# A two-layer gated attention trunk on one core: the third head pair's values move to another buffer, and VectorE instead of GpSimd scales the probabilities

## The chip, the cores and the metric

The kernel runs on one NeuronCore of a Trainium2 chip. The metric is the device time of the whole program in microseconds (us); lower is better. Engines are named as in the profile: PE (TensorE, matrix products; PEld is its weight load), DVE (VectorE), ACT (ScalarE), POOL (GpSimd), SP (the queue that issues the weight loads). Each engine works through its own instruction list in order, and an instruction waits until the semaphores it names have reached their counts.

## The reference: what is computed

Two layers act on 256 tokens of width 1024, in float32. Each layer is a half-step SwiGLU, a gated mixer, and another half-step SwiGLU. The mixer adds a pooling branch and an eight-head causal attention. The attention, cut to what matters:

```python
q = (rms_norm(q_lat, q_norm) @ w_uq).reshape(B, S, N_HEADS, QK_DIM)       # 128 + 64 rotary per head
kv = (rms_norm(kv_lat, kv_norm) @ w_ukv).reshape(B, S, N_HEADS, 128 + 128)
k_nope, v = kv[..., :128], kv[..., 128:]
for blk in range(S // 128):                                               # causal, 128 queries at a time
    s = (q_nope @ k_nope^T + q_rope @ k_rope^T) * QK_DIM ** -0.5
    p = softmax(where(mask, s, min))
    outs.append(p @ v[:, :k_end])
```

## The kernel before, in words

**Precision by splitting.** Every product is made of three passes over fp32r operands: high by high, high by low, low by high (`passes`). So each operand exists twice. ACT copies it rounded to fp32r (the high part, `high`, `split`), and DVE subtracts that from the original (the low part, `low`, `split`). Weights arrive in a ring of three slots `raw`, which ACT turns into `w_hi` and DVE into `w_lo`, one group `m` at a time (`split_mix(L, m)`); "split m" below is that step. A slot of `w_hi` is free again when PE has used the group three earlier.

**The attention by head pairs.** Eight heads are four pairs `p` = 0 to 3. For each pair PE makes the queries (`pair_queries`, parts QN and QRO) and the keys and values (`pair_keys`, parts KN and VV) in PSUM banks 2 to 5, one bank per part. ACT and DVE take each part out with `operands(L, p, part)`. PE then makes the scores (`pair_scores`, banks 6 and 7); DVE masks them and takes row maxima (`maxima`); ACT makes the exponentials and their row sums (`softmax`); `normalise` divides by the sums; PE transposes the probabilities into banks 0 and 1 (`turn_probs`); ACT and DVE copy these out (`probs`); PE multiplies by the values into bank 0 (`pair_values`); ACT and DVE copy the result to `oT` (`heads_out`). The rotary part of a query goes from PSUM to `xs` on ACT (`rope_copy`), is multiplied on POOL (`rope`), and goes on to ACT and DVE (part QRO).

**Order.** The lists of all engines are written out by hand and interleave these steps. The pieces of PE's list around the change are `pair_queries(2)`, `pair_keys(2)`, `turn_probs(0)`, `pair_scores(1)`, `pair_queries(3)`, `pair_values(0)`, `pair_keys(3)`, `turn_probs(1)`, `pair_scores(2)`, the first half of the pooling projection, `pair_values(1)`, its second half, `turn_probs(2)`, `pair_scores(3)`, and so on. Three waits of PE matter:

- `turn_probs(p)` waits for `prob_done`, count p+1 (`normalise(p)` is done), and for p above 0 also for `o_lo`, count p: DVE has read bank 0 in `heads_out(p-1)`.
- `pair_keys(3)` writes the values of pair 3 into bank 5, and first waits until DVE has taken the values of pair 2 out of it (`free(L, 3, VV)`).
- `pair_values(p)` waits for `prob_lo` and the low part of the values.

**Buffers.** `pair(p, part)` lies in `xT` for even p and in `pair1` for odd p. The values of pair 2 therefore overwrite those of pair 0, and ACT may copy them only when `pair_values(0)` is done (`pv_done`). `oT` holds the outputs of all eight heads; its last two heads are written by `heads_out(3)`, at the end of the attention.

Of the kernel before, what the change touches and what calls it, by code (L numbers as in the profile page):

```python
# [27 lines left out]
ALU = mybir.AluOpType  # L28
AX = mybir.AxisListType

P = 128
S, D, DEPTH = 256, 1024, 2
TB = S // P
KD = D // P
HEADS, NOPE, ROPE, VD = 8, 128, 64, 128
# [19 lines left out]
PAIRS = HEADS // 2  # L55
# [28 lines left out]
QN, QRO, KN, VV = range(4)  # L84

PART_ORDER = [(p, part) for p in range(2) for part in (QN, KN, VV, QRO)]
PART_ORDER += [(2, QN), (2, KN), (2, QRO), (3, QN), (2, VV), (3, KN), (3, QRO), (3, VV)]


GU_BANK, TR_BANK = 4, 6  # L90
# [49 lines left out]
def trunk(nc, x_in, positions, gains, ffn1_up, ffn1_down, w_in, b_gate, pool_maps, pool_scale,  # L140
          w_pool_proj, q_latent_norm, w_uq, kv_latent_norm, w_ukv, w_attn_proj, w_out,
          ffn2_up, ffn2_down, c_ident, c_causal, c_window, c_inv_count, c_rotary, out):
    with ExitStack() as ctx:
        def sb(name, shape, dt=F32):
            return ctx.enter_context(nc.sbuf_tensor(name, shape, dt))
# [17 lines left out]
        oT = sb("oT", [P, 2, HEADS, S], F32R)  # L163
# [27 lines left out]
        rot_t = rot[:, S:2 * S].rearrange("p (t c n) -> p t c n", t=TB, c=2)  # L191

        def pair(p, part):
            buf = (xT, pair1)[p % 2]
            return buf[:, :, 2 * part:2 * part + 2, :]

# [2 lines left out]
        LSQ, LMS, LRS = 6, 10, 14  # L199
        SMX, SNM, SSUM, SINV = 18, 22, 26, 28  # L200
        stat2 = sb("stat2", [P, 2, 16])
        half_neg, neg_one = sb("half_neg", [P, 2]), sb("neg_one", [P, 4])
        table_junk = sb("table_junk", [P, 1])
        pos_col_i, pos_col = sb("pos_col_i", [P, TB], I32), sb("pos_col", [P, TB])

# [249 lines left out]
        def _(pool):  # L455
# [2 lines left out]
                return pool.dma_start(dst, src.to_broadcast(list(dst.shape))).then_inc(landed, 16)  # L458

            pool.memset(half_neg[:, :], -0.5).then_inc(exponent_set, 1)  # L460
            pool.memset(neg_one[:, :], -1.0).then_inc(exponent_set, 1)
            def load_tables():

                pool.wait_ge(first_landed[1][3], 16)
# [59 lines left out]
                tensor(angle[:, :], angle[:, :], sign, ALU.mult)  # L524
                rot_op(pool.tensor_copy(window[:, :], window_f))

            def normalise(L, p):
                row, st = scores[:, p % 2, :], stat2[:, p % 2, :]
                pool.wait_ge(exp_done.sem, exp_done.upto(L, p + 1))
                pool.tensor_tensor(st[:, 12:16], st[:, 8:12], neg_one[:, :], ALU.pow).then_inc(inv_done.sem, 1)  # L530
                pool.wait_ge(inv_done.sem, inv_done.upto(L, p + 1))
                for cols, i, n in ((slice(0, 2 * S), 12, S), (slice(2 * S, 3 * S), 14, P)):
                    v = row[:, cols].rearrange("p (h n) -> p h n", h=2)
                    last = pool.tensor_tensor(v, v, st[:, i:i + 2].unsqueeze(2).to_broadcast([P, 2, n]), ALU.mult)
                last.then_inc(prob_done.sem, 1)

            def rope(L, p):
                both = rope_rows(p).rearrange("p (h n) -> p h n", h=2)
                pool.wait_ge(rope_in.sem, rope_in.upto(L, p + 1))
                pool.tensor_tensor(both, both, rot_f.unsqueeze(1).to_broadcast([P, 2, S]),  # L540
                                   ALU.mult).then_inc(rope_done.sem, 1)
# [15 lines left out]
                    pool.wait_ge(normed[h].sem, normed[h].upto(L, normed_count(s, TB - 1)))  # L557
                broadcast(gain[:, :], gains[bass.ds(L * 3 + s + 1, 1), :], gain_landed)

            pool.wait_ge(exponent_set, 2)  # L560
            def rest(L):

                broadcast(lat_gain[:, 0:QR], q_latent_norm[bass.ds(L, 1), :], latg_landed)
                broadcast(lat_gain[:, QR:QR + KVR], kv_latent_norm[bass.ds(L, 1), :], latg_landed)
                for t in range(TB):
                    broadcast(gates[:, t, :], b_gate[bass.ds(L, 1), :], bias_landed)
                next_gain(L, 0)
                second_half(L, 1)
                next_gain(L, 1)
                norm_rsqrt(L, 1)  # L570
                for i in range(2):
                    pool.wait_ge(lat_ms.sem, lat_ms.upto(L, i + 1))
                    rs = stat[:, LRS + 2 * i:LRS + 2 * i + 2]
                    rsqrt(rs, stat[:, LMS + 2 * i:LMS + 2 * i + 2], 2, lat_rstd)

                    pool.wait_ge(lat_rstd.sem, lat_rstd.upto(L, i + 1))
                    pool.tensor_tensor(rs, rs, stat[:, NRS:NRS + TB], ALU.mult).then_inc(lat_scale.sem, 1)
                rope(L, 0)
                rope(L, 1)
                normalise(L, 0)  # L580
                rope(L, 2)
                normalise(L, 1)
                rope(L, 3)
                normalise(L, 2)
                normalise(L, 3)
                second_half(L, 2)
                next_gain(L, 2)
                norm_rsqrt(L, 2)
# [32 lines left out]
        def _(act):  # L621
# [85 lines left out]
            def operands(L, p, which):  # L707
                for part in which:
                    src = psum[:, 2 + part, :]
                    if part == QRO:  # L710
                        high(L, rope_done, p + 1, flat(pair(p, part), 0), rope_rows(p), part_hi)
                        continue
                    if part == VV and p >= 2:

                        act.wait_ge(pv_done.sem, pv_done.upto(L, p - 1))
                    part_products(act, L, p, part)
                    act.activation(flat(pair(p, part), 0), src, ACT.Copy).then_inc(part_hi.sem, 1)
# [47 lines left out]
            def mixer(L):  # L765
# [46 lines left out]
                operands(L, 2, (QN, ))  # L812
                rope_copy(L, 2)
                split_mix(L, 22)
                operands(L, 2, (KN,))
                probs(L, 0)
                split_mix(L, 23)
                operands(L, 2, (QRO,))
                softmax(L, 1)
                operands(L, 3, (QN,))  # L820
                rope_copy(L, 3)
                operands(L, 2, (VV,))
                heads_out(L, 0)
                operands(L, 3, (KN,))
                split_mix(L, 24)
# [83 lines left out]
        def _(dve):  # L909
# [16 lines left out]
            def split_mix(L, m):  # L926
                if m < MIX_GROUPS:
                    split(L, (MIX0 + m) // RING, m % RING, m)
                else:
                    split(L, FFN2_0 // RING, m - MIX_GROUPS)  # L930
# [255 lines left out]
            def operands(L, p, which):  # L1186
                for part in which:
                    src = psum[:, 2 + part, :]
                    if part == QRO:
                        src = rope_rows(p)  # L1190
                    low(L, part_hi, part_count(p, part), flat(pair(p, part), 1), src, flat(pair(p, part), 0), part_lo)

            def maxima(L, p):
# [11 lines left out]
                dve.wait_ge(max_done.sem, max_done.upto(L, p + 1))  # L1205
                dve.tensor_scalar(st[:, 4:8], st[:, 0:4], -SCALE, None, ALU.mult).then_inc(bias_done.sem, 1)

            def probs(L, p):
                low(L, prob_hi, p + 1, small_T[:, 1, 0:3 * S], banks(0)[:, 0:3 * S], small_T[:, 0, 0:3 * S], prob_lo)

            def heads_out(L, p):
                o = oT[:, :, 2 * p:2 * p + 2, :]
                low(L, o_hi, p + 1, flat(o, 1), psum[:, 0, :], flat(o, 0), o_lo)
# [20 lines left out]
            def mixer(L):  # L1234
# [47 lines left out]
                operands(L, 1, (QRO,))  # L1282
                operands(L, 2, (QN,))
                split_mix(L, 22)
                operands(L, 2, (KN,))
                probs(L, 0)
                maxima(L, 1)
                split_mix(L, 23)
                operands(L, 2, (QRO,))
                operands(L, 3, (QN,))  # L1290
                operands(L, 2, (VV,))
                heads_out(L, 0)
                operands(L, 3, (KN,))
                split_mix(L, 24)
                probs(L, 1)
                maxima(L, 2)
                split_mix(L, 25)
                operands(L, 3, (QRO, VV))
                heads_out(L, 1)
                dve.wait_ge(gate_sig.sem, gate_sig.upto(L, 4 * TB))  # L1300
# [1 line left out]
                probs(L, 2)  # L1302
                maxima(L, 3)
                split_mix(L, 26)
                heads_out(L, 2)
                probs(L, 3)
                gate_a(L, 1)
# [408 lines left out]
```

## Time and profile before

| | |
|---|---|
| median of 3 runs | 1135.0 us (1133.81 to 1137.13) |
| the profiled execution: its time, and the span of its trace | 1135.97 us, 1134.2 us |
| PE busy in the span | 1114.0 us (98%) |
| DVE busy | 649.9 us (57%) |
| ACT busy | 538.0 us (47%) |
| POOL busy | 127.4 us (11%) |
| attention of layer 0, of layer 1 | about 282 to 345 us, about 838 to 901 us |

The span is the time from the first to the last instruction of the trace; the execution's own time is 1.8 us more. A busy share says how full an engine is, not whether it is waited for. The attention is done once in each layer, and the rows of the two layers repeat each other, so only those of layer 0 are shown.

### The profile page before, as it was taken

The page shows a single profiled execution, that of the slowest core. Times are in us where ns is not written, and L with a number is a line of the kernel's source. Part 1 is how long each engine was busy: PE and PEld are TensorE (multiplying, and loading weights), DVE is VectorE, ACT ScalarE, POOL GpSimd, SP SyncE. Part 2 cuts the span into 40 slices and gives each one's busy share as a digit, 9 for nine tenths or more (in the row PEclk, how much of TensorE's full clock was granted, in tenths as well). Part 3 has the DMA queues.
Part 4 walks back from the last instruction along what each step waited for, and adds up shares of the span by engine and source line. Part 5 has one row for each costly group of instructions (what it writes and reads, how often), then busy time and mean ns, then how long its engine had stood idle before and what let it go on. Part 6 is the DMA issues. An engine that isn't in the chain of part 4 may idle for free.

```text
span 1134.2 us, 14607 instructions
## 1 busy us (share of the span) xinstructions
PE 1114.0 (98%) x5472; PEld 937.6 (83%) x5472; DVE 649.9 (57%) x610; ACT 538.0 (47%) x615; POOL 127.4 (11%) x122
## 2 busy tenths in 40 slices
PE   7999999999999999999999999999999999999997
PEld 5788888988988888888878888888899888888886
DVE  4555455676776554544565545556568576454454
ACT  5444434554863443444444443446567435344442
POOL 4960000200230100000020000011002101000000
PEclk9999999999999999999999999999999999999999
DMA  9667554554544655556557565538435355655650
GB/s 301 229 221 248 190 185 153 191 189 125 189 149 149 202 187 186 184 185 191 186 203 258 184 193 185 185 102 278 141 129 196 121 180 185 201 185 185 188 181 37
DMA packets 140487, 208.59 MB, mean 184 GB/s; under 512 B 5185, under 2 KB 103617, under 8 KB 139937
## 3 DMA queue, kind: packets, MB, share of 16 engines
q1 hardware_dynamic: 137456, 196.69, 53.3%
q0 software_dynamic: 2128, 9.80, 2.6%
q10 hardware_dynamic: 864, 1.57, 0.4%
q8 instruction: 26, 0.43, 0.2%
q14 instruction: 13, 0.10, 0.0%
HBM read 207.00 MB, written 1.05 MB: 183 GB/s over the span
## 4 chain that ended last, share of the span: by engine, by line
PE 93%; DVE 3%; ACT 3%; POOL 1%; issue 0%; POOLq 0%; ACTq 0%; DVEq 0%
PE psum L1341 30%; PE psum L1343 30%; PE psum L1342 29%; PE psum L1409 2%; PE psum L1359 1%; DVE w_lo L917 1%; PE psum L1684 1%; ACT scores L735 1%; ACT w_hi L630 1%; ACT xs L723 0%; POOL xs L544 0%; DVE xT L917 0%; PE psum L1551 0%; ACT xT L650 0%; DVE stat L1203 0%
## 5 line engine op out<-in xcount | busy, mean ns | idle before, releaser
L917 DVE TENSOR_TENSOR w_lo<-raw,w_hi 128x2048 fp32r<-128x2048 f32 (+6 forms) x212 | 436.6, 2066 | 266.6 <-ACT w_hi L630 264.3
L630 ACT ACTIVATE w_hi<-raw 128x2048 fp32r<-128x2048 f32 (+5 forms) x204 | 355.2, 1748 | 181.6 <-PE psum L1343 166.0
L1341 PE MATMUL psum<-w_hi,xT 128*128 128x512 f32 (+2 forms) x992 | 389.7, 393 | 7.4 <-DVE scores L1086 4.7
L1343 PE MATMUL psum<-w_hi,xT 128*128 128x512 f32 (+2 forms) x992 | 383.5, 387 | 0.0
L1342 PE MATMUL psum<-w_lo,xT 128*128 128x512 f32 (+2 forms) x992 | 382.8, 386 | 0.0
L1341 PEld LDWEIGHTS psum<-w_hi,xT 128*128 128x128 f32 x992 | 186.8, 188 | 44.6 <-DVE w_lo L917 9.2
L1343 PEld LDWEIGHTS psum<-w_hi,xT 128*128 128x128 f32 x992 | 186.5, 188 | 37.5
L1342 PEld LDWEIGHTS psum<-w_lo,xT 128*128 128x128 f32 x992 | 186.9, 188 | 34.4
L1341 PE MATMUL psum<-w_hi,small_T 128*128 128x512 f32 x352 | 137.6, 391 | 0.0
L1343 PE MATMUL psum<-w_hi,small_T 128*128 128x512 f32 x352 | 137.0, 389 | 0.0
L1342 PE MATMUL psum<-w_lo,small_T 128*128 128x512 f32 x352 | 137.0, 389 | 0.0
L650 ACT ACTIVATE small_T<-psum 128x512 fp32r<-128x512 f32 (+1 forms) x52 | 32.9, 632 | 173.7 <-PE psum L1409 161.4
L917 DVE TENSOR_TENSOR small_T<-psum,small_T 128x512 fp32r<-128x512 f32 (+1 forms) x52 | 38.1, 732 | 97.7 <-ACT small_T L650 97.4
L679 ACT ACTIVATE scores<-psum,stat 128x256 f32<-128x256 f32 x88 | 41.6, 474 | 102.9 <-PE psum L1343 102.9
L544 POOL TENSOR_TENSOR xs<-x,gain 128x512 f32<-128x512 f32 x12 | 20.7, 1733 | 593.6 <-DVE x L911 583.9
L1343 PEld LDWEIGHTS psum<-w_hi,small_T 128*128 128x128 f32 x352 | 66.1, 188 | 13.8
L1342 PEld LDWEIGHTS psum<-w_lo,small_T 128*128 128x128 f32 x352 | 66.1, 188 | 13.5
L1341 PEld LDWEIGHTS psum<-w_hi,small_T 128*128 128x128 f32 x352 | 66.1, 188 | 13.5
L1086 DVE SCALAR_TENSOR_TENSOR scores<-psum,stat,scores 128x256 f32<-128x256 f32 x88 | 42.0, 480 | 37.3 <-ACT scores L679 37.3
L650 ACT ACTIVATE xT<-psum 128x512 fp32r<-128x512 f32 x32 | 19.2, 600 | 59.5 <-PE psum L1359 59.4
L917 DVE TENSOR_TENSOR xT<-psum,xT 128x512 fp32r<-128x512 f32 x44 | 30.1, 688 | 29.4 <-ACT xT L650 27.3
L1341 PE MATMUL psum<-latT,w_hi 128*128 128x256 f32 x104 | 29.7, 286 | 0.0
(173 smaller groups left out, 947.0 us busy)
## 6 DMA issues: line engine op xcount, KB each, us to landing
raw<-ffn_up_dram SPq DMA_DIRECT2D x172, 512.0 KB, 4.7
raw<-ffn_down_dram SPq DMA_DIRECT2D x44, 1024.0 KB, 4.9
raw<-w_in_dram SPq DMA_DIRECT2D x20, 1024.0 KB, 5.2
raw<-w_attn_proj_dram SPq DMA_DIRECT2D x8, 1024.0 KB, 5.1
raw<-w_out_dram SPq DMA_DIRECT2D x8, 1024.0 KB, 5.0
raw<-w_uq_dram SPq DMA_DIRECT2D x8, 576.0 KB, 4.1
gates<-b_gate_dram POOLq DMA_DIRECT2D x4, 1024.0 KB, 8.0
raw<-w_ukv_dram SPq DMA_DIRECT2D x8, 512.0 KB, 4.0
```

Source lines behind the costliest of these rows:

```text
L544: pool.tensor_tensor(xs[:, t, half(h)], x[:, t, half(h)], gain[:, half(h)], ALU.mult).then_inc(normed[h].sem, 1)
L630: last = act.activation(dst(w_hi[:, r, :]), src(raw[:, r, :]), ACT.Copy)
L650: act.activation(dst, src, ACT.Copy).then_inc(done.sem, 1)
L679: act.activation(silu_sb[:, t, :], psum[:, GU_BANK + t, 0:CH], ACT.Silu, scale=rstd(t)).then_inc(silu_done.sem, 1)
L735: last = act.activation(row[:, cols], src, ACT.Exp, scale=SCALE, bias=st[:, 4 + i:5 + i], accum_out=st[:, 8 + i:9 + i])
L917: return dve.tensor_tensor(dst, a, b, ALU.subtract)
L1086: dve.scalar_tensor_tensor(out=act_sb[:, t, :], in0=psum[:, GU_BANK + t, CH:2 * CH], scalar=rstd(t), in1=silu_sb[:, t, :], op0=ALU.mult, o ...
L1341: nc.tensor.matmul(dst, a_hi, b_hi, start=first, stop=False)
L1342: nc.tensor.matmul(dst, a_hi, b_lo, start=False, stop=False)
L1343: return nc.tensor.matmul(dst, a_lo, b_hi, start=False, stop=last)
L1359: last = nc.tensor.transpose(dst[:, k * P:(k + 1) * P], src[:, k * P:(k + 1) * P], ident[:, :])
L1409: last = nc.tensor.transpose(psum[:, TR_BANK, k * S + t * P:k * S + (t + 1) * P], act_sb[:, t, k * P:(k + 1) * P], ident[:, :])
```

## The change

The values of pair 2 get a place of their own in the last two heads of `oT`, and are copied out of PSUM together with the keys of pair 2, with no wait for `pair_values(0)`. `normalise` moves from POOL's list to DVE's: POOL had one power of -1 over 4 columns and two broadcast products (512 and 256 columns); DVE has one reciprocal over 4 columns and four products by a per-row scalar (256, 256, 128, 128 columns). In each layer that is four calls. Everything that issues a DMA is as before.

```diff
-PART_ORDER += [(2, QN), (2, KN), (2, QRO), (3, QN), (2, VV), (3, KN), (3, QRO), (3, VV)]
+PART_ORDER += [(2, QN), (2, KN), (2, VV), (2, QRO), (3, QN), (3, KN), (3, QRO), (3, VV)]
...
         def pair(p, part):
+            if (p, part) == (2, VV):
+                return oT[:, :, HEADS - 2:HEADS, :]
             buf = (xT, pair1)[p % 2]
...
 # POOL
-            def normalise(L, p):
-                row, st = scores[:, p % 2, :], stat2[:, p % 2, :]
-                pool.wait_ge(exp_done.sem, exp_done.upto(L, p + 1))
-                pool.tensor_tensor(st[:, 12:16], st[:, 8:12], neg_one[:, :], ALU.pow).then_inc(inv_done.sem, 1)
-                pool.wait_ge(inv_done.sem, inv_done.upto(L, p + 1))
-                for cols, i, n in ((slice(0, 2 * S), 12, S), (slice(2 * S, 3 * S), 14, P)):
-                    v = row[:, cols].rearrange("p (h n) -> p h n", h=2)
-                    last = pool.tensor_tensor(v, v, st[:, i:i + 2].unsqueeze(2).to_broadcast([P, 2, n]), ALU.mult)
-                last.then_inc(prob_done.sem, 1)
...
-                rope(L, 0)
-                rope(L, 1)
-                normalise(L, 0)
-                rope(L, 2)
-                normalise(L, 1)
-                rope(L, 3)
-                normalise(L, 2)
-                normalise(L, 3)
+                for p in range(PAIRS):
+                    rope(L, p)
...
 # ACT
-                    if part == VV and p >= 2:
+                    if part == VV and p == 3:
                         act.wait_ge(pv_done.sem, pv_done.upto(L, p - 1))
...
                 split_mix(L, 22)
-                operands(L, 2, (KN,))
+                operands(L, 2, (KN, VV))
                 probs(L, 0)
...
                 rope_copy(L, 3)
-                operands(L, 2, (VV,))
                 heads_out(L, 0)
...
 # DVE
+            def normalise(L, p):
+                row, st = scores[:, p % 2, :], stat2[:, p % 2, :]
+                dve.wait_ge(exp_done.sem, exp_done.upto(L, p + 1))
+                dve.reciprocal(st[:, 12:16], st[:, 8:12]).then_inc(inv_done.sem, 1)
+                dve.wait_ge(inv_done.sem, inv_done.upto(L, p + 1))
+                for i, cols in enumerate(ROWS):
+                    last = dve.tensor_scalar(row[:, cols], row[:, cols], st[:, 12 + i:13 + i], None, ALU.mult)
+                last.then_inc(prob_done.sem, 1)
...
                 split_mix(L, 22)
-                operands(L, 2, (KN,))
+                normalise(L, 0)
+                operands(L, 2, (KN, VV))
                 probs(L, 0)
                 maxima(L, 1)
                 split_mix(L, 23)
+                normalise(L, 1)
                 operands(L, 2, (QRO,))
                 operands(L, 3, (QN,))
-                operands(L, 2, (VV,))
                 heads_out(L, 0)
...
                 split_mix(L, 25)
+                normalise(L, 2)
                 operands(L, 3, (QRO, VV))
                 heads_out(L, 1)
...
                 split_mix(L, 26)
+                normalise(L, 3)
                 heads_out(L, 2)
```

DVE's list of before, layer 0, from the rotary queries of pair 1 (`pair<-xs`) to the start of `maxima(1)`; the row with 1024 columns is split 22, `xT<-psum,xT` are the low parts of pair 2's queries and keys, `small_T` is `probs(0)`:

```order
L917 TENSOR_TENSOR pair<-xs,pair 128x512
L917 TENSOR_TENSOR xT<-psum,xT 128x512
L917 TENSOR_TENSOR w_lo<-raw,w_hi 128x1024
L917 TENSOR_TENSOR xT<-psum,xT 128x512
L917 TENSOR_TENSOR small_T<-psum,small_T 128x768
L1200 TENSOR_TENSOR psum<-psum,causal 128x2x128
```

The same place in the changed kernel, where `oT<-psum,oT` is the low part of pair 2's values:

```order
L901 TENSOR_TENSOR pair<-xs,pair 128x512
L901 TENSOR_TENSOR xT<-psum,xT 128x512
L901 TENSOR_TENSOR w_lo<-raw,w_hi 128x1024
L1195 RECIPROCAL stat<-stat 128x4
L1198 TENSOR_SCALAR scores<-scores,stat 128x256 x2
L1198 TENSOR_SCALAR scores<-scores,stat 128x128 x2
L901 TENSOR_TENSOR xT<-psum,xT 128x512
L901 TENSOR_TENSOR oT<-psum,oT 128x512
L901 TENSOR_TENSOR small_T<-psum,small_T 128x768
L1184 TENSOR_TENSOR psum<-psum,causal 128x2x128
```

`normalise(0)` now stands behind split 22 on DVE, and the copy of the values stands ahead of `probs(0)`.

ACT's list of before, layer 0, from the last exponentials of `softmax(1)` through the queries of pair 3 (`pair<-psum`), its rotary copy (`xs<-psum`), the values of pair 2 (`xT<-psum`), `heads_out(0)` (`oT<-psum`) and the keys of pair 3 to split 24:

```order
L735 ACTIVATE scores,stat<-psum,stat 128x128 x2
L717 ACTIVATE pair<-psum 128x512
L723 ACTIVATE xs<-psum 64x256 x4
L717 ACTIVATE xT<-psum 128x512
L650 ACTIVATE oT<-psum 128x512
L717 ACTIVATE pair<-psum 128x512
L630 ACTIVATE w_hi<-raw 128x2048
```

The same place in the changed kernel:

```order
L720 ACTIVATE scores,stat<-psum,stat 128x128 x2
L702 ACTIVATE pair<-psum 128x512
L708 ACTIVATE xs<-psum 64x256 x4
L635 ACTIVATE oT<-psum 128x512
L702 ACTIVATE pair<-psum 128x512
L615 ACTIVATE w_hi<-raw 128x2048
```

The copy of pair 2's values is gone from between `rope_copy(3)` and `heads_out(0)`.

DVE's list of the changed kernel from split 25 through `normalise(2)`, the rotary queries (`pair<-xs`) and values (`pair<-psum`) of pair 3, and `heads_out(1)`:

```order
L901 TENSOR_TENSOR w_lo<-raw,w_hi 128x2048
L1195 RECIPROCAL stat<-stat 128x4
L1198 TENSOR_SCALAR scores<-scores,stat 128x256 x2
L1198 TENSOR_SCALAR scores<-scores,stat 128x128 x2
L901 TENSOR_TENSOR pair<-xs,pair 128x512
L901 TENSOR_TENSOR pair<-psum,pair 128x512
L901 TENSOR_TENSOR oT<-psum,oT 128x512
```

Before, the reciprocal and the four products were not there, and the other four rows followed one another.

## Rows read from the trace of the kernel before

**Rows 1.** The page, part 1: busy us, share of the span, instructions.

```profile
PE 1114.0 (98%) x5472; PEld 937.6 (83%) x5472; DVE 649.9 (57%) x610; ACT 538.0 (47%) x615; POOL 127.4 (11%) x122
```

**Rows 2.** What PE waited for, whole span: us in total, times, longest.

```profile
PE psum L1341 <- DVE xT L917: 2.3, 3, 1.0
...
PE psum L1551 <- POOL scores L534: 1.3, 2, 0.7
```

**Rows 3.** Timeline, PE around `turn_probs(0)`: start, us; idle before, releaser.

```profile
302.55 0.28 PE L1343 MATMUL psum<-w_hi,latT 128*128 128x256 f32 x1
303.49 0.85 PE L1551 MATMUL psum<-ident,scores 128*128 128x128 f32 x6 [0.66 <-POOL scores L534]
```

**Rows 4.** Timeline, POOL: `normalise(0)` and `rope(2)`.

```profile
300.56 1.09 POOL L530 TENSOR_TENSOR stat<-stat,neg_one 128x4 f32<-128x4 f32 x1 [5.86 <-ACT scores L735]
301.73 1.61 POOL L534 TENSOR_TENSOR scores<-scores,stat 128x512 f32<-128x512 f32 x2
303.30 1.28 POOL L540 TENSOR_TENSOR xs<-xs,rot 128x512 f32<-128x512 f32 x1
```

**Rows 5.** Timeline, split 22 on ACT and on DVE.

```profile
302.42 1.06 ACT L630 ACTIVATE w_hi<-raw 128x1024 fp32r<-128x1024 f32 x1
...
303.51 2.15 DVE L917 TENSOR_TENSOR w_lo<-raw,w_hi 128x1024 fp32r<-128x1024 f32 x1 [1.05 <-ACT w_hi L630]
```

**Rows 6.** Timeline, `rope(0)` on POOL, and split 18 on DVE.

```profile
287.62 1.29 POOL L540 TENSOR_TENSOR xs<-xs,rot 128x512 f32<-128x512 f32 x1 [58.10 <-ACT xs L723]
...
288.66 1.33 DVE L917 TENSOR_TENSOR w_lo<-raw,w_hi 128x1024 fp32r<-128x1024 f32 x1 [3.35 <-ACT w_hi L630]
```

**Rows 7.** Groups of DVE by form: busy us, mean ns of one, idle before.

```profile
L1200 DVE TENSOR_TENSOR psum<-psum,causal 128x256 f32<-128x256 f32 x8 | 3.5, 433 | 3.7 <-PE psum L1343 3.7
...
L1206 DVE TENSOR_SCALAR stat<-stat 128x4 f32<-128x4 f32 x8 | 1.4, 170 | 0.3
L1143 DVE TENSOR_SCALAR xs<-psum,stat 128x64 f32<-128x64 f32 x4 | 0.9, 277 | 0.0
...
L914 DVE TENSOR_TENSOR xs<-xs,rot 128x128 f32<-128x128 f32 x2 | 0.6, 292 | 0.1
```

**Rows 8.** Timeline, PE and DVE around the values of pair 3.

```profile
312.88 0.28 PE L1343 MATMUL psum<-latT,w_lo 128*128 128x256 f32 x1
314.20 0.39 PE L1341 MATMUL psum<-w_hi,latT 128*128 128x256 f32 x1 [1.04 <-DVE xT L917]
...
315.74 0.82 PE L1551 MATMUL psum<-ident,scores 128*128 128x128 f32 x6
...
313.45 0.69 DVE L917 TENSOR_TENSOR xT<-psum,xT 128x512 fp32r<-128x512 f32 x1 [0.93 <-ACT xT L717]
```

**Rows 9.** Timeline, DVE: start of `maxima(1)`, and split 23.

```profile
307.10 0.43 DVE L1200 TENSOR_TENSOR psum<-psum,causal 128x256 f32<-128x256 f32 x1
...
309.04 2.28 DVE L917 TENSOR_TENSOR w_lo<-raw,w_hi 128x2048 fp32r<-128x2048 f32 x1
```

**Rows 10.** Timeline, ACT from `rope_copy(3)` to split 24.

```profile
311.24 1.56 ACT L723 ACTIVATE xs<-psum 64x256 f32<-64x256 f32 x4
312.82 0.60 ACT L717 ACTIVATE xT<-psum 128x512 fp32r<-128x512 f32 x1
313.32 0.59 ACT L650 ACTIVATE oT<-psum 128x512 fp32r<-128x512 f32 x1
...
314.27 1.93 ACT L630 ACTIVATE w_hi<-raw 128x2048 fp32r<-128x2048 f32 x1
```

**Rows 11.** Timeline, DVE: split 24, rotary queries of pair 3, `heads_out(1)`.

```profile
316.23 2.29 DVE L917 TENSOR_TENSOR w_lo<-raw,w_hi 128x2048 fp32r<-128x2048 f32 x1 [0.89 <-ACT w_hi L630]
...
323.46 0.69 DVE L917 TENSOR_TENSOR pair<-xs,pair 128x512 fp32r<-128x512 f32 x1
...
324.71 0.68 DVE L917 TENSOR_TENSOR oT<-psum,oT 128x512 fp32r<-128x512 f32 x1
```

**Rows 12.** Timeline, PE: `turn_probs(2)`.

```profile
326.15 0.87 PE L1551 MATMUL psum<-ident,scores 128*128 128x128 f32 x6
```

More of the change, by code:

```diff
@@ L201, in trunk @@
         stat2 = sb("stat2", [P, 2, 16])
-        half_neg, neg_one = sb("half_neg", [P, 2]), sb("neg_one", [P, 4])
+        half_neg = sb("half_neg", [P, 2])
         table_junk = sb("table_junk", [P, 1])
@@ L460, in _ @@
             pool.memset(half_neg[:, :], -0.5).then_inc(exponent_set, 1)
-            pool.memset(neg_one[:, :], -1.0).then_inc(exponent_set, 1)
             def load_tables():
@@ L558, in next_gain @@
                 broadcast(gain[:, :], gains[bass.ds(L * 3 + s + 1, 1), :], gain_landed)
-            pool.wait_ge(exponent_set, 2)
+            pool.wait_ge(exponent_set, 1)
             def rest(L):
```

## The prediction, written before the changed kernel ran

> **What bounds the kernel now.** I read the busy shares first: PE is busy 98% of the span, so time is lost or won only where PE stands still [rows 1]. The list of PE's waits then says what this change can touch. PE waits twice, once per layer, for GpSimd's scaled probabilities, 0.66 us each, and three times for DVE to take something out into `xT`; the longest two of these, 1.04 us each, are the values of pair 2 [rows 2]. The timelines put both in place: the first stands ahead of `turn_probs(0)` [rows 3], the second inside `pair_keys(3)`, ahead of its value products [rows 8]. Everything else on POOL, DVE and ACT is either behind PE or has to be proved late by working through their queues, which is what I do next. Both layers show the same pattern, so I work one layer and double it.
>
> **What the change removes.** The wait in `pair_keys(3)` goes: the values of pair 2 will be copied some six us before they are asked for. Its price is start to start. Without it the products would have followed at 312.88 + 0.12 = 313.00 (the pitch of such products is 0.12) instead of 314.20, which is 1.20. The twelve of them took 315.74 - 314.20 = 1.54 where twelve at pitch take 1.44, so the restart cost 0.10 more. Gain 1.30 per layer [rows 8]. On POOL, 1.09 + 1.61 us of work go away per pair [rows 4]; POOL is not waited for again, so this is worth nothing by itself. ACT loses one copy of 0.50 (start to start) between `rope_copy(3)` and split 24 and gains it back ahead of `probs(0)`, where ACT will be waiting for PE anyway [rows 10].
>
> **What the change adds: the first stall.** DVE works in order, and `normalise(0)` stands behind split 22. Split 22 cannot start before ACT has made its high part, which ends at 303.48, and it starts at 303.51 [rows 5]. By then POOL had already finished `normalise(0)`, at 301.73 + 1.61 = 303.34 [rows 4], and PE went on at 303.49 [rows 3]. In the new order the probabilities are ready only at 303.51 + (split 22) + N, with N the length of `normalise` on DVE.
>
> Split 22 took 2.15 us, beside `rope(2)` on POOL from 303.30 to 304.58 [rows 4, 5]. The same instruction took 1.33 as split 18 [rows 6]. In the new kernel `rope(2)` no longer queues behind `normalise(0)`. It starts when its input is copied, about 302.5, and ends about 303.8, so only 0.26 us overlap split 22. Split 18 overlapped `rope(0)` by as much (287.62 + 1.29 = 288.91 against 288.66) and still took 1.33 [rows 6]. I take 1.33. The Trainium skill ("SBUF — State Buffer", Terms) says that DVE and GpSimd share a port pair which one of them holds for a whole instruction while the other fully blocks; this fits the 2.15 of split 22, but by it split 22 would also lose these 0.26 us, which makes the sum about 0.5 us larger over two layers, and the row of split 18 does not bear that out.
>
> An instruction with no wait starts about 0.08 before the end of the one ahead (307.10 and its followers on DVE step so), so `normalise(0)` starts at 304.76.
>
> N is not in the trace. The reciprocal over 4 columns I take as the nearest row, a TENSOR_SCALAR over 4 columns, 0.17, plus 0.04 until its own semaphore lets the products go: 0.21. For the products the nearest rows are a product by a per-row scalar of 64 columns, 0.277, and mask additions of 256 columns from PSUM, 0.433; 128 columns from SBUF took 0.292 [rows 7]. I take the middle, 0.36, for 256 columns and 0.28 for 128. Start to start that is 0.28 + 0.28 + 0.20 + 0.28 = 1.04, so N = 1.25. Low end: all four at 0.277, N = 1.1. High end: 0.433 and 0.35, N = 1.5, and a reciprocal three times as long as that row gives 1.7; if it cost as much as POOL's power, 1.09 [rows 4], N would be 2.3. The Trainium skill ("VectorE: DVE Perf Modes", the perf-mode tier table) says that a fp32 tensor_scalar within SBUF runs at two elements per cycle; an estimate from that page is N = 1.0 and a sum of 4.1 us in place of the one below.
>
> PE starts 0.06 after DVE ends (313.45 + 0.69 = 314.14 against 314.20 [rows 8]). So `turn_probs(0)` starts at 304.76 + 1.25 + 0.06 = 306.07 where it was 303.49: **2.58 later** (1.33 + N). Nothing of PE's can move ahead of it, and nothing hides it. The 0.66 us wait is not removed but becomes about 3.2.
>
> **After it.** Minus 1.30 for the values leaves PE 1.28 late (0.03 + N) at `turn_probs(1)`, 317.02. That step needs two things. `maxima(1)` follows PE's scores and starts at 307.10 + 2.58; split 23 follows at 309.04 + 2.58 = 311.62 and takes 2.20 start to start [rows 9]; `normalise(1)` runs 313.82 to 315.07, the rotary queries and queries take 0.60 each, and `heads_out(0)` (0.68) ends at 316.87. PE could go at 316.93: just in time, by 0.09. Any N above 1.34 makes a small third stall here.
>
> **The second stall, at `turn_probs(2)`.** Here `o_lo` is what counts. ACT's chain from `softmax(1)` over `rope_copy(3)` to split 24 is gapless [rows 10]; it starts 2.58 later and is 0.50 shorter, so split 24 is 2.08 later on ACT and on DVE, where it starts at 318.31, because DVE waited for it before too (0.89 idle) [rows 11]. From there DVE has no gap up to the rotary queries of pair 3 at 323.46, now 325.54. Ahead of them now stands `normalise(2)` (its exponentials are done by then), N - 0.08 = 1.17 more, so `heads_out(1)` starts at 324.71 + 2.08 + 1.17 = 327.96, ends at 328.64, and PE can go at 328.70. It was 326.15 [rows 11, 12]: **2.55 later** (0.05 + 2N), where PE itself would only have been 1.28 late. The cover was 326.15 - 325.39 - 0.06 = 0.70, and it is used up. At `turn_probs(3)` split 26 and `normalise(3)` end about 337.7 and `heads_out(2)` about 338.3, where PE arrives at about 339.1: no stall. The rest of the layer follows PE, and nothing later absorbs a delay, since PE had no other wait there.
>
> **Sum.** 2.55 per layer, 5.1 for both. The profiled execution had a span of 1134.2 and a time of 1135.97, 0.97 above the median of the runs. The new span would be 1139.3, and the median 1135.0 + 5.1 = **1140.1**, or 0.45% slower. About 0.3% (3.4 us) is what a measurement of this kernel tells from no change. With N from 1.1 to 1.7 the cost is 4.5 to 6.9: 1139.5 to 1141.9.
>
> **The rivals.**
> - *Only the first stall counts.* If DVE makes up 1.3 us before `heads_out(1)` (say ACT reaches split 24 earlier than its gapless chain allows), the cost is 2 x 1.28 = 2.6 us: 1137.6, no measurable change. For it speaks that my cover of 0.70 rests on a chain of some fifteen steps; against it that these steps have no gaps now. Chance 0.15.
> - *Faster.* Both waits of PE vanish and DVE is in time. That gives 1.30 + 0.82 (303.49 against 302.55 + 0.12 [rows 3]) per layer, 4.2 us: 1130.8. It decides at `turn_probs(0)`: the change wins as soon as the probabilities are ready less than 1.30 after 303.49, at 304.79, with `heads_out(1)` in time as well. Split 22 alone ends at 304.84, so it needs ACT to deliver split 22 over 1.2 us earlier, and ACT's list ahead of that point is unchanged. Chance 0.05.
> - *The port stays in the way.* If split 22 still takes 2.15, 0.82 is added per layer: 6.7 us, 1141.7. The row of split 18 speaks against it. Chance 0.06.
> - *A slow reciprocal.* With N = 2.3 the cost is 4.65 per layer, 1144.3. Only the power on another engine points that way. Chance 0.05.
> - *The moves change nothing* because the in-order view is wrong somewhere: 1135. Chance 0.04.
>
> My own case keeps 0.65.
>
> **How the numbers follow.** Slower by over 0.3% means above 1138.4: my case nearly whole (0.62), the port and the reciprocal (0.11), minus what run-to-run spread takes: 0.70. Within 0.3%: the first rival, the last, and the low tail of mine: 0.24. Faster: 0.06. The range takes in the first rival's upper half and the port's case, 1137.3 to 1142.1.
>
> **What would show it.** The page of the changed kernel should show DVE's split 22 at about 1.33 us, PE's wait ahead of `turn_probs(0)` at about 3.2 us and released by DVE's `scores`, no wait inside `pair_keys(3)`, next to none at `turn_probs(1)`, and about 1.2 us at `turn_probs(2)` released by DVE's `oT`, in both layers. PE's waits on POOL's `scores` go from 1.3 us to none. If the products turn out at 0.28 or less for 256 columns, N is 1.1 or less and the cost falls toward 4; if split 24 on DVE is less than 2.08 late, the second stall shrinks. The prediction is wrong in sign only if `turn_probs(0)` starts before 304.8.

## The result, and the profile after

The changed kernel took 1144.68 us (median of 4 runs, 1142.86 to 1145.51) against 1134.4 for the kernel before: ratio 1.0083, interval 1.007 to 1.0095. Run again later beside the kernel before, six runs of the same kernel gave 1141.39, ratio 1.005 (1.0038 to 1.0063). The forecast was 1140.1 and 1.0045, with 1142.1 as the upper end. The direction was right and the cost too small, and two sets of runs of one kernel differ by 3 us. TensorE's clock turns out to be behind the first, and, as far as profiles and granted clocks show, behind the second too.

The profile page of the changed kernel, its span and part 1, the row that answers to [rows 1]:

```profile
span 1143.7 us, 14620 instructions
...
PE 1118.3 (98%) x5472; PEld 942.6 (82%) x5472; DVE 656.1 (57%) x650; ACT 537.1 (47%) x615; POOL 104.5 (9%) x97
```

PE's busy time rose by 4.3 us although it executes the same 5472 products. That is not waiting: some products took longer. What PE waited for, in total, times, longest [rows 2]:

```profile
PE psum L1547 <- DVE scores L1198: 6.5, 2, 3.3
PE psum L1337 <- DVE scores L1070: 4.5, 2, 2.3
PE psum L1547 <- DVE oT L901: 2.4, 2, 1.2
```

The first row is `turn_probs(0)` in both layers, the second a wait in each layer's first feed-forward, which was there before (4.7), the third `turn_probs(2)`. The wait for POOL's `scores` (1.3) and the two waits of 1.04 for `xT` in `pair_keys(3)` are gone; the page still has one wait for `xT`, 0.98 long, but it stands at 12 us, in the first feed-forward. PE's timeline at `turn_probs` 0 to 3 of layer 0 (start, us, idle before) [rows 3, 8, 12]:

```profile
307.88 1.44 PE L1547 MATMUL psum<-ident,scores 128*128 128x128 f32 x6 [3.26 <-DVE scores L1198]
320.38 0.82 PE L1547 MATMUL psum<-ident,scores 128*128 128x128 f32 x6
332.04 0.84 PE L1547 MATMUL psum<-ident,scores 128*128 128x128 f32 x6 [1.19 <-DVE oT L901]
342.38 0.82 PE L1547 MATMUL psum<-ident,scores 128*128 128x128 f32 x6
```

The six transposes of `turn_probs(0)` took 1.44 us where they took 0.85 [rows 3]. The windows around it (width, PE busy, PEld, DVE, ACT, POOL, then the granted clock, DMA share, GB/s) say why:

```profile
306.00:308.00 2.00, 0.12 (x1) 0.15 (x2) 1.97 (x7) 0.37 (x1) 0.00 (x0) 0.99 1.16 337
308.00:309.00 1.00, 1.00 (x7) 1.00 (x6) 0.93 (x2) 0.00 (x0) 0.00 (x0) 0.50 0.53 172
309.00:310.00 1.00, 1.00 (x7) 1.00 (x6) 0.00 (x0) 0.65 (x1) 0.00 (x0) 0.50 1.06 412
310.00:311.00 1.00, 1.00 (x6) 1.00 (x6) 0.80 (x1) 1.00 (x2) 0.00 (x0) 0.50 1.03 401
311.00:312.00 1.00, 1.00 (x10) 1.00 (x8) 0.15 (x1) 1.00 (x2) 0.00 (x0) 0.80 0.11 41
312.00:313.00 1.00, 1.00 (x11) 1.00 (x10) 0.00 (x0) 0.48 (x1) 0.00 (x0) 1.00 0.00 0
```

After the idle 3.26 us the granted clock is 0.50, the 1.2 GHz level, for over 3 us, and then 1.00 again, the 2.4 GHz level. Products of 256 columns follow one another there at 0.21 us instead of 0.12. VectorE's and GpSimd's timelines at the same place [rows 4 to 6]:

```profile
304.25 1.27 POOL L531 TENSOR_TENSOR xs<-xs,rot 128x512 f32<-128x512 f32 x1 [7.78 <-ACT xs L708]
...
305.29 1.31 DVE L901 TENSOR_TENSOR w_lo<-raw,w_hi 128x1024 fp32r<-128x1024 f32 x1 [1.05 <-ACT w_hi L615]
306.52 0.17 DVE L1195 RECIPROCAL stat<-stat 128x4 f32<-128x4 f32 x1
306.72 1.01 DVE L1198 TENSOR_SCALAR scores<-scores,stat 128x256 f32<-128x256 f32 x4
```

Split 22 takes 1.31, and `normalise(0)` runs from 306.52 to 307.73, N = 1.21.

**A measure free of the beginning.** The first 40 us vary by up to 4 us between the profiles (part 4 of the experiments says what they show of it), so I measure each attention from VectorE's first reduction in `maxima(0)` to the one in `maxima(3)`. Timeline of VectorE, the kernel before:

```profile
297.50 0.69 DVE L1203 TENSOR_REDUCE stat<-psum 128x2 f32<-128x512 f32 x1
...
330.59 0.69 DVE L1203 TENSOR_REDUCE stat<-psum 128x2 f32<-128x512 f32 x1
```

and the changed kernel:

```profile
299.29 0.69 DVE L1187 TENSOR_REDUCE stat<-psum 128x2 f32<-128x512 f32 x1
...
336.44 0.69 DVE L1187 TENSOR_REDUCE stat<-psum 128x2 f32<-128x512 f32 x1
```

That is 33.09 before and 37.15 after, 4.06 more per layer (4.07 in layer 1), 8.1 in both. The first row already lies 1.79 later, before any `normalise` or any part of pair 2 has run. So the 9.5 us between the two spans are 8.1 of the change and 1.8 of the beginning, less 0.4 elsewhere. In the second profile of the changed kernel the same reduction starts at 295.18, earlier than in the kernel before, and the attention takes 37.12.

### The profile page after: what moved, and what is told of

Read it like the earlier page. It is cut to its first block, busy times and chain, and to the rows that moved or that the text cites. A ratio compares the mean times of both kernels' runs of the same rounds, so it can differ in the third digit from the quotient of the medians.

```text
span 1143.7 us, 14620 instructions
## 1 busy us (share of the span) xinstructions
PE 1118.3 (98%) x5472; PEld 942.6 (82%) x5472; DVE 656.1 (57%) x650; ACT 537.1 (47%) x615; POOL 104.5 (9%) x97
## 4 chain that ended last, share of the span: by engine, by line
PE 91%; DVE 4%; ACT 3%; POOL 1%; issue 1%; POOLq 0%; ACTq 0%; DVEq 0%
PE psum L1337 29%; PE psum L1339 29%; PE psum L1338 29%; PE psum L1405 2%; DVE w_lo L901 2%; PE psum L1355 1%; ACT w_hi L615 1%; PE psum L1680 1%; ACT scores L720 1%; PE psum L1547 0%; ACT xs L708 0%; POOL xs L535 0%; DVE stat L1187 0%; DVE scores L1198 0%; ACT xT L635 0%
```

## The experiments

All times are medians, with ratios to the kernel before run beside them; there were three such groups (the first four rows, the next four, the last three). "Attention" is the measure above, from one profile of each kernel, layer 0; layer 1 gives the same within 0.05, but for normalise only (4.48).

| run | median us | ratio (interval) | attention | against before |
|---|---|---|---|---|
| values only | 1135.21 | 1.0001 (0.9992 to 1.0011) | 33.1 | 0.0 |
| normalise only | 1143.92 | 1.0072 (1.0059 to 1.0085) | 37.7 | +4.6 |
| first early | 1134.91 | 1.0 (0.999 to 1.001) | 33.1 | 0.0 |
| busy wait | 1141.55 | 1.0054 (1.0041 to 1.0068) | 35.6 | +2.5 |
| second early | 1141.35 | 1.0053 (1.0038 to 1.0067) | 35.74 | +2.65 |
| changed kernel again | 1141.39 | 1.005 (1.0038 to 1.0063) | 37.12 | +4.03 |
| idle only | 1141.31 | 1.0052 (1.0039 to 1.0065) | 36.79 | +3.70 |
| all early | 1134.13 | 0.9984 (0.9973 to 0.9996) | 31.90 | -1.19 |
| feed-forward busy | 1133.85 | 0.999 (0.9981 to 0.9999) | 33.09 | 0.0 |
| half busy | 1142.12 | 1.006 (1.0046 to 1.0074) | 35.57 | +2.48 |
| early and busy | 1131.31 | 0.9965 (0.9953 to 0.9977) | 31.91 | -1.18 |

My theory (A in the expectations) was that TensorE, having stood idle behind VectorE's queue, runs on at its lower level and so pays again. The rivals were that the lower clock has another source (B), and that the longer beginning belongs to the changed kernel (C).

**1. The two halves of the change.** Values only: the buffer, `PART_ORDER` and the operand lists of the change, with `normalise` left on GpSimd.

```diff
 # the kernel before, with
+            if (p, part) == (2, VV):
+                return oT[:, :, HEADS - 2:HEADS, :]
...
-                operands(L, 2, (KN,))
+                operands(L, 2, (KN, VV))
...
-                operands(L, 2, (VV,))
```

> The values of pair 2 in the last heads of oT, normalise left on GpSimd. If the values' wait alone is worth what was worked out (1.30 us per layer) and nothing takes it back, the span falls by 2.6 us. Working the queues through says less: GpSimd's normalise(2) follows softmax(2), which follows ScalarE's chain and comes only 0.50 earlier, so turn_probs(2) can start only 0.5 earlier and PE waits there about 0.8. Expected: no wait inside pair_keys(3), the 0.66 wait at turn_probs(0) as before, a new wait of about 0.8 at turn_probs(2), and 1.0 to 1.2 us less than before in all, about 1133.3. The rival (full gain) gives 1131.8. The clock stays full in both attentions. If the slower first 30 us of the changed kernel's profile (1.8 us) belong to the changed buffer, they show here too.

Measured: no gain at all. PE's waits in its profile:

```profile
PE psum L1551 <- POOL scores L536: 3.0, 4, 0.9
...
PE psum L1551 <- DVE oT L918: 0.4, 2, 0.2
```

Of the 1.30 us per layer, 0.38 are given back by `turn_probs(1)`, where PE waits 0.22, and the other 0.9 by `turn_probs(2)`, where it waits 0.85 for `normalise(2)`. I had expected half a microsecond to remain, because ScalarE's chain loses one copy. It does not remain: in that trace the moved low part of the values stands ahead of `probs(0)` on VectorE and sends `maxima(1)` off 0.5 later, which cancels the copy that ScalarE lost: counted from `maxima(0)`, ScalarE starts split 24 at 16.82 where it started at 16.77.

Normalise only: the changed kernel with the values back in `xT`.

> normalise on VectorE in the changed kernel's places, the values of pair 2 still in xT with their wait for pair_values(0). Theory A (the stall behind split 22, then TensorE at its lower clock level for about 3 us because it had stood idle): turn_probs(0) 2.6 later than before, the scores after it another 1.6 slower, the wait inside pair_keys(3) about as long as before or 0.2 longer, and turn_probs(2) about 4.5 later: 9 us in all, about 1143.5, so moving the values makes nearly no difference once normalise has moved. Theory B (the lower clock comes from something else in the changed kernel or from the run): no lower clock here, 2.6 to 3.0 per layer, 1140.

Measured as forecast by theory A, with the lower clock in it. The wait inside `pair_keys(3)` is back, up to 1.2 long. So the whole cost comes from moving `normalise`, and moving the values saves 0.6 of it in layer 0 (4.63 against 4.06) and 0.4 in layer 1 (4.48 against 4.07).

**2. Is it the idle time?** Busy wait: TensorE gets something to do while it waits.

```diff
                 wait(gate_biased, L, 4 * TB)
+                for _ in range(13):
+                    nc.tensor.matmul(psum[:, 0, :], small_T[:, 0, 0:P], small_T[:, 0, P:5 * P], start=True, stop=True)
                 turn_probs(L, 0)
```

> The changed kernel with 13 extra products of 512 columns into a free PSUM bank ahead of turn_probs(0), about 3.0 us of work inside the 3.26 us that PE would wait. Their result is overwritten. Theory A: turn_probs(0) starts when it did in the changed kernel, the clock stays full, turn_probs(0) to maxima(1) takes 3.6 us where the changed kernel took 5.2, and the whole is 3.1 us faster than the changed kernel: about 1141.5, or 1139.7 with a start like that of the kernel before. Theory B (the clock falls for another reason than the idle time): half clock as before and 1144.7, or more if the extra products come late.

PE's timeline at `turn_probs(0)`, and the windows behind it:

```profile
305.40 0.87 PE L1547 MATMUL psum<-ident,scores 128*128 128x128 f32 x6 [0.24 <-DVE scores L1198]
```

```profile
305.00:308.00 3.00, 2.76 (x24) 2.61 (x24) 2.39 (x5) 1.69 (x2) 0.00 (x0) 1.00 0.90 266
308.00:311.00 3.00, 3.00 (x27) 3.00 (x27) 2.01 (x7) 1.44 (x2) 0.00 (x0) 1.00 0.25 95
```

The clock stays at 1.00 and the attention costs 2.5 more than before instead of 4.06. The useful work starts no earlier; only the idle time was filled. Theory B would have left the cost.

The median does not show these 3.1 us. It is 1141.55, 2.4 below normalise only (1143.92), which ran in the same group, but no better than the changed kernel again (1141.39). The profile of this run has two stretches of lower clock outside the attention, behind the feed-forward waits at 28 and 588 us (granted 0.50 at 30 to 32 us, 0.55 at 590 to 592 us), and the second profile of the changed kernel has none. So the filling is shown to keep the clock up behind this wait; that it shortens the whole program is not shown.

Half busy: the same with `range(6)`.

> The changed kernel with 6 extra products ahead of turn_probs(0), so that PE is idle there about 1.9 us instead of 3.26. The 13 of the busy-wait run kept the clock up altogether. Theory A gives a case between: either the lower level still comes in all or some executions (1141.4 as for the changed kernel), or it stays away and the time is that of the busy-wait run less nothing, 2.5 per layer over before. By the idle stretch of 2.1 us at the feed-forward, which brought it in some executions only, I expect a mixture: 1140 to 1141. The start of turn_probs(0) and the second stall stay where they were.

```profile
303.75 0.87 PE L1547 MATMUL psum<-ident,scores 128*128 128x128 f32 x6 [1.81 <-DVE scores L1198]
```

Idle 1.81, and no lower clock in either attention (+2.48). The median was nevertheless that of the changed kernel, above what I expected: its profile has a stretch of lower clock at 586 us instead, outside the attention. That profile is of an execution of 1140.52, and three of the other four took over 1142; whether the lower level came in their attentions is not known.

Idle only: the kernel before, with nothing moved and one wait more.

```diff
                 wait(gate_biased, L, 4 * TB)
+                mix_weights(L, 22)
                 turn_probs(L, 0)
```

> The kernel before with one wait added on PE ahead of turn_probs(0): for the low part of weight group 22, which VectorE has ready at 305.66 us of the trace of before. No work is added or moved anywhere. PE stands idle about 2.9 us there instead of 0.66. Theory A: idle time alone brings the lower clock level, turn_probs(0) 2.2 late and maxima(1) 3.8 late, nothing made up later, 7.6 us in all, about 1142.7. Theory B (the lower clock comes with VectorE's normalise or with the moved buffer): 2.2 per layer, 1139.5, clock full.

```profile
303.27 1.51 PE L1551 MATMUL psum<-ident,scores 128*128 128x128 f32 x6 [2.92 <-DVE w_lo L917]
```

```profile
304.00:306.00 2.00, 2.00 (x11) 2.00 (x10) 0.34 (x1) 1.18 (x2) 0.00 (x0) 0.50 0.62 191
```

This separates the causes most sharply: no `normalise` on VectorE, no new buffer, PE idle 2.92 us, and the transposes take 1.51. The delay of the wait is 2.25 (from `maxima(0)`, 8.24 at `turn_probs(0)` against 5.99), the attention costs 3.70. The other 1.45 is the clock, granted 0.50 in the window shown. The median is 5.6 us over that of before and not 7.4, as the kernel before has stretches of lower clock elsewhere in many of its executions (part 4).

**3. The stalls.** First early: `normalise(L, 0)` moved on VectorE from behind split 22 to ahead of `operands(L, 1, (QRO,))`.

> The changed kernel with normalise(0) moved up on VectorE, ahead of the rotary queries of pair 1 and of split 22. Theory A: the probabilities are ready before PE asks, no wait at turn_probs(0), full clock all through, no wait inside pair_keys(3); heads_out(1) still stands behind normalise(2), so PE waits about 1.2 at turn_probs(2). That is 0.9 less than before per layer, 1132.6. Theory B: the lower clock still shows in the scores of pair 1 and the time stays near 1136 or above.

Half of this came true. The wait at `turn_probs(0)` and the lower clock are gone, but the gain of 0.9 per layer is not there: PE waits for `heads_out` twice.

```profile
312.26 0.85 PE L1547 MATMUL psum<-ident,scores 128*128 128x128 f32 x6 [0.75 <-DVE oT L901]
...
323.96 0.85 PE L1547 MATMUL psum<-ident,scores 128*128 128x128 f32 x6 [1.19 <-DVE oT L901]
```

I had foreseen only the second. VectorE's list is without a gap there, so `normalise` costs its 1.2 us wherever it stands, unless what PE waits for goes ahead of it.

Second early: the changed kernel, `heads_out(1)` ahead of the operands of pair 3.

```diff
 # VectorE
                 normalise(L, 2)
+                heads_out(L, 1)
                 operands(L, 3, (QRO, VV))
-                heads_out(L, 1)
...
 # ScalarE
                 softmax(L, 2)
+                heads_out(L, 1)
                 operands(L, 3, (VV,))
-                heads_out(L, 1)
```

> The changed kernel with heads_out(1) moved ahead of the rotary queries and values of pair 3 on VectorE, and ahead of the copy of those values on ScalarE. If the second stall (1.19 us at turn_probs(2)) is the queue ahead of heads_out(1), as worked out, it goes: 1.2 to 1.3 less per layer, 2.5 us under the changed kernel, about 1142. The first stall and the lower clock after it stay. The rival, that normalise(2) itself or the transposes' other wait sets turn_probs(2), leaves the wait and the time as they are, 1144.5.

The second stall is gone, which confirms its cause. The attention is 1.38 shorter (35.74 against 37.12), 1.19 of it the stall and nearly all of the rest a cheaper stretch of lower clock behind the first (`turn_probs(0)` to `maxima(1)` 5.75 against 5.93). The medians do not show the 2.8 us: that of the changed kernel beside it is 1141.39, this one 1141.35. Between the two profiles the difference can be placed. This one has a stretch of lower clock between 580 and 600 us (granted 0.91 over the twenty) that the other has not and that costs 1.6, and its `maxima(0)` starts 0.48 later; 2.8 less these two is 0.7, the difference of the spans (1138.9 and 1139.6). The other executions have no profile; their granted clocks are 0.992 to 0.995, against 0.994 to 0.996.

**4. Where the spread comes from.** The changed kernel again:

> The changed kernel itself, again, for a second profile. Theory A says that what belongs to the change is 4.1 us per layer (2.6 of first stall, 1.6 of lower clock, less 1.3, plus 1.2 of second stall), 8.2 in all: ratio about 1.0072, about 1143.2, and that the 1.8 us by which the first 40 us were longer in its first profile are chance: the first maxima(0) then lies anywhere between 294 and 299 us. Theory C, that the slower beginning belongs to the changed kernel, puts maxima(0) at 298.5 again and the ratio at 1.0083 or above.

The first reduction of `maxima(0)` starts at 295.18 against 299.29 and the attention costs what it did. Theory C falls: the longer beginning does not belong to the kernel. What theory A had for the ratio, 1.0072, was missed; it was 1.005. The mean granted clock is 0.996 in five of these six executions, in the four of the first set 0.993 or 0.994. The first profile shows two stretches at its beginning for it, the first behind three short waits:

```profile
12.00 0.50 PE L1337 MATMUL psum<-w_hi,xT 128*128 128x512 f32 x1 [0.98 <-DVE xT L901]
13.68 0.50 PE L1337 MATMUL psum<-w_hi,xT 128*128 128x512 f32 x1 [0.71 <-DVE w_lo L901]
14.88 0.80 PE L1337 MATMUL psum<-w_hi,xT 128*128 128x512 f32 x1 [0.17 <-DVE w_lo L901]
```

```profile
14.00:16.00 2.00, 1.83 (x6) 1.12 (x5) 1.43 (x3) 0.00 (x0) 0.50 (x1) 0.61 1.09 345
...
32.00:34.00 2.00, 2.00 (x7) 1.54 (x5) 1.52 (x2) 1.82 (x1) 1.90 (x2) 0.50 0.94 284
```

The second profile has 1.00 in all these windows. The two stretches cost about 3.0 of the 4.1 us between the beginnings; 0.86 is there before the first (this product starts at 14.88, in the second profile at 14.02). Why all four executions of the first set were so and none of the second stays open.

All early: first early, second early, and `heads_out(0)` directly behind `softmax(1)` on ScalarE and `normalise(1)` on VectorE.

> The changed kernel with normalise(0) ahead of the rotary queries of pair 1 (as in the first-early run) and heads_out(0) and heads_out(1) right behind softmax on ScalarE and right behind normalise on VectorE. In the first-early run PE waited 0.75 at turn_probs(1) and 1.19 at turn_probs(2), both for VectorE's oT. Expected: the first of these waits gone, turn_probs(2) about 1.3 earlier than in the first-early run with 0.5 to 0.9 of wait left, behind normalise(2), and 2.6 us less than before in all, about 1132.6. If VectorE's and ScalarE's chain from split 24 on is what really sets the pace, turn_probs(2) does not come earlier and the time is that of before.

The attention is 1.19 shorter than before, with 0.94 of wait left at `turn_probs(2)`. The whole gained 1.6 us instead of 2.6, and the profile shows a place where the rest can have gone. PE at the second chunk of the first feed-forward of layer 1, and the windows there:

```profile
584.41 0.47 PE L1337 MATMUL psum<-w_hi,xT 128*128 128x512 f32 x1 [2.12 <-DVE scores L1070]
```

The granted clock was 1.00 up to 584, 0.76 in the two microseconds from there, 0.50 in the next two, 0.89 in the next, then 1.00. The first-early run has the same wait of 2.12 at 584.07 and keeps 1.00 throughout. So an idle stretch of 2.1 us brings the lower level in one execution and not in another. Eleven of the profiles have this wait unfilled at two places, 2.04 to 2.56 long, at about 29 and 588 us, and the lower level came behind 10 of the 22.

Feed-forward busy: the kernel before, with that wait filled.

```diff
+                if f == 0:
+                    for _ in range(8):
+                        nc.tensor.matmul(psum[:, 7, :], small_T[:, 0, 0:P], small_T[:, 0, P:5 * P], start=True, stop=True)
                 chunk(1)
```

> The kernel before with 8 extra products of 512 columns into a free PSUM bank (1.8 us) ahead of the second chunk of the first feed-forward of each layer, where PE stands idle 2.6 and 2.1 us for scores at 29 and 586 us of the trace of before. Profiles so far show a stretch of lower clock of about 3 us behind those waits in some executions and none in others, with all else alike. Theory A (each idle stretch of 2 us or more of PE may bring the lower level, 1.5 us each time, and this makes the spread between executions): no lower clock behind the two places, the fastest run as before (1133.6), the median falls to about 1134, and most runs within 1 us of each other. The rival, that the spread comes from transfers at the start or from elsewhere, leaves the median at 1135.3 and the spread as it is.

Ten of its eleven runs lie between 1133.57 and 1134.44; the sixteen of the kernel before beside it between 1133.52 and 1137.77, median 1135.34. The stretch from 26 to 36 us, the kernel before and then this one:

```profile
26.00:36.00 10.00, 7.44 (x26) 5.68 (x25) 7.87 (x5) 4.30 (x4) 9.60 (x6) 0.83 0.84 274
```

```profile
26.00:36.00 10.00, 9.71 (x45) 7.71 (x44) 8.17 (x6) 5.56 (x5) 9.46 (x8) 1.00 0.92 309
```

The fastest run is the same, and those above 1134.5 are all but gone (one, 1136.15, is left unexplained). The granted clocks of the single executions point the same way. Of the 56 of the kernel before in the three groups, the 20 with a mean of 0.999 took 1133.5 to 1134.8 us, the 21 with 0.998 or 0.997 took 1135.0 to 1136.0, and the 14 with 0.996 took 1136.6 to 1137.8 and the one with 0.994 took 1138.7: steps of about the price of one stretch.

Early and busy puts the two together:

> The all-early kernel with the 8 extra products of the feed-forward run. All-early saved 1.2 us per layer within the attention in its trace and lost 1.4 of it to a stretch of lower clock behind the idle 2.1 us at 584 us. With that place kept busy: 2.4 us under the kernel with the same filling, 1131.6, and a ratio to before of 0.996 to 0.997. If the lower clock at 584 us had another cause, it stays and the ratio is 0.998 as for all-early.

1131.31, all six runs within 0.9 us: 2.5 under the kernel before with the same filling (1133.85), which is twice the 1.19 of the attention. This is the fastest kernel of the study.

## Why the prediction was wrong

- **What the move of `normalise(0)` costs at `turn_probs(0)`: right.** Forecast 2.58 later. From `maxima(0)` it starts 8.59 later where it started 5.99 later: 2.60. Split 22 took 1.31 (forecast 1.33, and no loss to GpSimd's `rope(2)`, which overlapped it by 0.23), N was 1.21 (forecast 1.25). One reading of mine was loose: waiting for the end of `rope(2)` at 304.58 and taking 1.33 after it would have made 2.40 of the old split 22, not its 2.15. The idle time was 3.26 (forecast about 3.2). The Trainium skill's rule of two elements per cycle ("VectorE: DVE Perf Modes", the perf-mode tier table) gave an estimate of N = 1.0; the trace does not bear it out, with 1.21.
- **No wait in `pair_keys(3)`, none at `turn_probs(1)`: right.**
- **The second stall at `turn_probs(2)`: right in place and cause.** Forecast about 1.2 of idle, released by `oT`; measured 1.19, and taken away by the second-early run. The start, 4.10 later than before, is the forecast 2.55 plus 1.55.
- **"Nothing of PE's can move ahead of it, and nothing hides it ... becomes about 3.2": here is the fault.** I charged an idle stretch of 3.2 us with its own length and no more. TensorE came out of it at the 1.2 GHz level and stayed there over 3 us. The missing term is 1.55 per layer, 3.1 in both, and 5.1 + 3.1 = 8.2 against 8.1 measured in the attentions. This 1.55 is itself read from the delay; what makes it more than a remainder is that the busy-wait run removed it alone (4.06 to 2.5), and the idle-only run produced it without the change (1.45). None of my rivals had it. The trace of before had a warning: the clock is 0.83 between 26 and 36 us, behind an idle 2.56. The Trainium skill ("TensorE: Matmul & The Clock Gate", Part 1) says that the array runs at half rate when it has not been busy, and that the moment of the switch depends on a phase that differs between runs. The traces agree with the first: 0.50 behind 3.26 and 2.92 of idle time in both attentions of all five profiles that have such a wait. A phase shows in none of them; what they do show is that nearly equal waits, of 2.04 to 2.56, were followed by 0.50 in 10 cases of 22.
- **The rest of the gap to 1144.7 does not belong to the change.** 1134.4 + 8.1 = 1142.5 lies between the medians of the two sets, 1144.7 and 1141.4. In the profiled executions they differ mostly by where else the clock fell.
- **Two near hits are luck.** The second set's ratio of 1.005 is close to the forecast 1.0045, but its attentions cost 8.1 and not 5.1. The rival with a slow reciprocal named 1144.3, close to the first set's 1144.68, but the reciprocal took 0.17 and N was 1.21.
- **The gain of 1.30 from the values: right as a term of this sum.** It must not be read as what that half of the change is worth: alone it is worth nothing (values only), beside the moved `normalise` 0.4 to 0.6.
- **"About 0.3% is what a measurement can tell": too narrow for single sets.** The two sets of the changed kernel are 0.33% apart in their ratios. One stretch of lower clock costs about 1.5 us, 0.13%, and the profiles show none to two of them outside the attention.

## What to carry to other kernels

Work moved to an idle-looking engine lands in a queue: ask what stands ahead of it at the moment it is needed (here a weight split that itself waits for ScalarE), and what PE waits for that now stands behind it. When TensorE is the bound, price an idle stretch by its length and by what the lower clock can cost behind it, here about 1.5 us: always behind the stretches of 2.9 us and more, sometimes behind those of 2.0 to 2.6. Filling a wait with throwaway products kept the clock up behind it and, at the feed-forward, steadied the run times; look at the granted clock of the whole trace afterwards, as the next such wait may pay in its place. A removed wait is worth only what the next one, a microsecond behind, leaves of it.

## What the runs showed that I had not expected

- TensorE's clock after idle time: the 0.50 level came behind 3.26 and 2.92 us in both attentions of every profile with such a wait (10 of 10), behind 2.04 to 2.56 us at the feed-forwards in 10 of 22, and not behind 1.81 us in the one profile that has it (two attentions) nor behind the 1.2 us at `turn_probs(2)`. Short waits are not safe for that: in one profile of the changed kernel it came behind 0.98, 0.71 and 0.17 us within four microseconds, and in another (second early) it did not come behind 0.98 and 0.72. Each stretch in the attention and at the feed-forwards cost 1.3 to 1.6 us.
- The run-to-run spread of the kernel before (1133.5 to 1137.8) is mostly this clock: filling two waits with 1.8 us of products each brought the median from 1135.34 to 1133.85, with the fastest run unchanged, and the times of single executions follow their granted clocks.
- A float32 product by a per-row scalar within SBUF, 2 x 256 and 2 x 128 columns, took 1.01 us together, and a reciprocal over 4 columns 0.17, no more than another small instruction; GpSimd took 1.61 for its two broadcast products and 1.09 for its power [rows 4].
